# Two-layer hybrid decoder step: all heads two per bisection round, top-k rounds inside the projection, bias table flipped by DMA

## What is computed

```python
def mixer_ab(hn, attend, conv_buf, h0, w_in, w_out, conv_w, conv_b, wa, ba, wx, bx, lam):
    q, k, v, qi, ki, wi, g, xr = split_cols(hn @ w_in, AB_SPLITS)
    ...
    attn = attend(q, k, v, qi, ki, wi)
    rg, new_buf, h_last = rglru_branch(g, xr, conv_buf, h0, conv_w, conv_b, wa, ba, wx, bx, lam)
    return jnp.concatenate([attn, rg], axis=-1) @ w_out, k, v, ki, h_last, new_buf

def select_topk(scores, q_pos, k_pos, topk):
    admissible = k_pos[None, None, :] <= q_pos[None, :, None]
    _, idx = lax.top_k(jnp.where(admissible, scores, -jnp.inf), topk)
    ...

def gathered_attention(q, k_sel, v_sel, sel_pos, valid, q_pos, rel_bias):
    ...
    bias = rel_bias[t5_bucket(q_pos[None, :, None] - sel_pos)].astype(jnp.float32)
    logits = jnp.where(valid[:, :, None, None, :], logits + bias, -jnp.inf)
    p = jax.nn.softmax(logits, axis=-1).astype(v_sel.dtype)
    out = jnp.einsum('bqkgj,bqjkd->bqkgd', p, v_sel)

def rglru_branch(g, xr, buf, h0, conv_w, conv_b, wa, ba, wx, bx, lam):
    xc, new_buf = causal_dwconv(xr, buf, conv_w, conv_b)
    r = sigmoid(xb @ wa + ba); i = sigmoid(xb @ wx + bx)
    log_a = -RG_C * r * jax.nn.softplus(-lam.astype(jnp.float32))
    u = jnp.sqrt(-jnp.expm1(2.0 * log_a)) * (i * xc.astype(jnp.float32))
    hs, h_last = linear_recurrence(jnp.exp(log_a), u, h0.astype(jnp.float32))
    return jax.nn.gelu(g) * hs.astype(g.dtype), new_buf, h_last.astype(h0.dtype)
```

## Time and profile before

| | us |
|---|---|
| three executions | 1347.97, 1351.44, 1353.28; median 1351.44 |
| the profiled execution | 1351.15, its span 1349.4 |
| TensorE busy | 1256.8 (93%) |
| VectorE busy | 702.3 (52%) |
| ScalarE busy | 470.2 (35%) |
| GpSimd busy | 193.0 (14%) |

### The profile page before, as it was taken

The page is one execution under the profiler, slowest core; times in us unless marked ns, Lnnn a source line. Parts: engine busy times, 40 slices in busy tenths (PEclk is TensorE's granted clock), DMA queues, the critical chain, the costliest instruction groups (busy, mean ns, idle before and its releaser), DMA issues.

```text
span 1349.4 us, 24444 instructions
## 1 busy us (share of the span) xinstructions
PE 1256.8 (93%) x9991; PEld 1213.2 (90%) x9993; DVE 702.3 (52%) x1279; ACT 470.2 (35%) x548; POOL 193.0 (14%) x285
## 2 busy tenths in 40 slices
PE   5998994795999999999999999999999999999995
PEld 5878993563899999999999999999899999999994
DVE  5267786767347555555522244644755555552323
ACT  5243235451224434343322234332543343432110
POOL 0111001106303111111100010030411111110000
PEclk9999997696799999999999999999999999999998
DMA  7143301002222222222222332112122222222211
GB/s 271 64 149 123 132 33 46 1 2 65 68 93 70 89 91 93 93 93 93 87 89 109 102 125 94 64 64 93 63 94 93 93 93 93 93 86 87 86 60 63
DMA packets 25992, 118.17 MB, mean 88 GB/s; under 512 B 7720, under 2 KB 9192, under 8 KB 13904
## 3 DMA queue, kind: packets, MB, share of 16 engines
q1 hardware_dynamic: 21184, 105.50, 22.4%
q0 software_dynamic: 2048, 10.54, 2.3%
q10 hardware_dynamic: 2704, 1.35, 0.4%
HBM read 113.91 MB, written 3.46 MB: 87 GB/s over the span
## 4 chain that ended last, share of the span: by engine, by line
PE 70%; DVE 2%; POOL 1%; ACT 1%; issue 0%; DVEq 0%
PE ps L814 22%; PE ps L815 22%; PE ps L817 22%; POOL xl L1802 1%; PE ps L831 1%; PE ps L950 1%; PE ps L947 1%; PE ps L948 1%; PE ps L1209 0%; DVE acc L1240 0%; DVE vtc L1765 0%; DVE yt L1794 0%; PE ps L1121 0%; DVE rstd L1244 0%; DVE xn L1244 0%
## 5 line engine op out<-in xcount | busy, mean ns | idle before, releaser
L814 PE MATMUL ps<-xh,w_h 128*128 128x260 f32 x1792 | 471.4, 284 | 7.9 <-POOL xl L1802 7.8
L815 PE MATMUL ps<-xl,w_h 128*128 128x260 f32 x1792 | 469.6, 283 | 0.0
L817 PE MATMUL ps<-xh,w_l 128*128 128x260 f32 x1792 | 361.0, 283 | 0.0
L814 PEld LDWEIGHTS ps<-xh,w_h 128*128 128x128 f32 x1792 | 339.4, 189 | 9.1 <-issue 7.6
L815 PEld LDWEIGHTS ps<-xl,w_h 128*128 128x128 f32 x1792 | 338.8, 189 | 0.1
L1233 DVE TENSOR_TENSOR w_l<-w_raw,w_h 128x2048 fp32r<-128x2048 f32 (+1 forms) x94 | 211.6, 2251 | 166.4 <-ACT w_h L503 166.2
L817 PEld LDWEIGHTS ps<-xh,w_l 128*128 128x128 f32 x1792 | 277.1, 189 | 0.0
L815 PE MATMUL ps<-hl,w_h 128*128 128x260 f32 x704 | 183.9, 282 | 0.0
L503 ACT ACTIVATE w_h<-w_raw 128x2048 fp32r<-128x2048 f32 (+1 forms) x50 | 92.3, 1846 | 262.2 <-PE ps L817 242.4
L814 PE MATMUL ps<-hh,w_h 128*128 128x260 f32 x704 | 183.4, 282 | 0.0
L947 PE MATMUL ps<-xh,w_h 128*128 128x260 f32 x448 | 128.9, 309 | 14.1 <-DVE xl L1253 12.5
(11 more groups left out here) (298 smaller groups left out, 1406.3 us busy)
## 6 DMA issues: line engine op xcount, KB each, us to landing
w_raw<-in_wstream SPq DMA_DIRECT2D x86, 1024.0 KB, 4.8
w_raw<-in_wstream SPq DMA_DIRECT2D x8, 768.0 KB, 4.2
res<-in_x_t SPq DMA_DIRECT2D x4, 520.0 KB, 8.3
out_y<-yt SPq DMA_DIRECT2D x8, 260.0 KB, 2.2
tabf<-bias_by_distance SPq DMA_DIRECT2D x1, 2048.0 KB
wm<-in_sgu_w ACTq DMA_DIRECT2D x1, 512.0 KB, 3.6
sb_b<-in_sgu_b ACTq DMA_DIRECT2D x1, 512.0 KB, 4.2
out_f<-ost SPq DMA_DIRECT2D x2, 198.0 KB, 4.6
```

Of the source, the lines that this page charges most:

```text
L814: pe.matmul(out[h], wh, hi[h], start=(first and k == 0), stop=False)
L815: pe.matmul(out[h], wh, lo[h], start=False, stop=False)
L817: ins = pe.matmul(out[h], wl, hi[h], start=False, stop=(last and k == nk - 1))
```

## The change

- `ROUND`: rounds 9 to 24 have two heads each, 25 to 31 none. The wait for the logits of head 31 after the bisection goes.
- `p_work` on TensorE makes the next pair's logits first, then the turns and values.
- Rounds 0 to 7 get three matmuls on unused data behind the count (`warm`), into a PSUM bank that nobody reads.
- The shares of the recurrence move from rounds 2 to 5 to rounds 9 to 12, with ScalarE's rates; its root moves to round 17.
- All 48 top-k rounds lie inside groups 4 to 9. The page columns are split: their first half is made in group 6. The values are turned in group 9, step 12, and copied ahead of that group's last evacuation.
- The decay constants move from group 5 to group 1.
- The bias table is flipped by DMA: `fneg` is written to DRAM eight times per head, and sixteen reads fetch eight rows each, so the eight products, their copies, `flip` and `tabf` go. GpSimd no longer waits for the table at its start, nor for the gates ahead of its mask copies.

```diff
-        for rnd in range(17, 33):
-            ROUND[rnd] = (rnd - 1,)
+        for rnd in range(17, 25):
+            ROUND[rnd] = (2 * rnd - 18, 2 * rnd - 17)
...
-            sp.wait_ge(f_ev, 2)
-            sp.dma_start(scratch.ap(), fneg[:]).then_inc(d_scr, 16)
...
-                if s == 2:
-                    sp.wait_ge(d_scr, 16)
-                    sp.dma_start(tabf[:], bass.AP(scratch.ap().tensor, 0, [[1, P], [640, 8], [1, SEQ]])).then_inc(d_scr, 16)
+                if s == 3:
+                    sp.wait_ge(f_ev, 2)
+                    for h in range(2):
+                        sp.dma_start(bass.AP(scratch.ap().tensor, h * 8 * 640, [[2 * 8 * 640, 4], [640, 8], [1, 640]]),
+                                     fneg[4 * h:4 * h + 4, :].rearrange("p (a c) -> p a c", a=1).broadcast_to((4, 8, 640)))\
+                            .then_inc(d_scr, 16)
+                if s == 5:
+                    sp.wait_ge(d_scr, 32)
+                    for r in range(0, P, 8):
+                        sp.dma_start(tab[r:r + 8], bass.AP(scratch.ap().tensor, P - 1 - r,
+                                                           [[639, 8], [8 * 640, 8], [1, SEQ]])).then_inc(d_tabs, 16)
...
+                if g == 1:
                     act.wait_ge(sp_z, 1)
                     act.activation(lamt[:, 1, :], lamt[:, 0, :], ACT.Exp, scale=-1.0).then_inc(sp_e, 1)
...
-                    if g in (1, 2) and step % 4 == 3:
-                        table(4 * (g - 1) + step // 4)
...
+                if 9 <= rnd < 13:
+                    rates(rnd - 9)
+                if rnd == 17:
+                    roots()
...
+                if g == 9 and step == 12:
+                    turn_values()
...
             def p_work(rnd):
 
+                for i in heads(rnd + 1):
+                    if i % 2 == 0:
+                        p_pair(i // 2)
                 for i in heads(rnd - 1):
                     p_turn(i)
                 for i in heads(rnd - 2):
...
-                for i in heads(rnd + 1):
-                    if i % 2 == 0:
-                        p_pair(i // 2)
+            def warm():
+
+                for n in range(3):
+                    pe.matmul(ps[:, 3, :], sameb[:], pickb[NCH - 1][:], start=True, stop=True)
+
+            pe.wait_ge(topk_done, 3)
             for rnd in range(32):
                 count(rnd)
+                if rnd < 8:
+                    warm()
                 p_work(rnd)
...
-            rounds = {4: (0, 0, 3), 5: (4, 4, 2), 6: (4, 4, 2), 7: (4, 4, 2), 8: (0, 0, 0), 9: (4, 5, 0)}
+            rounds = {4: (0, 0, 3), 5: (4, 6, 2), 6: (4, 5, 2), 7: (4, 6, 3), 8: (0, 0, 2), 9: (4, 3, 0)}
...
-                if g == 5:
+                if g == 1:
                     decay_constants()
...
+                if g == 9:
+                    dve.wait_ge(vn_tr, 1)
+                    dve.wait_ge(d_kvi, 48)
+                    dve.tensor_copy(vn[:].rearrange("p n c -> p (n c)"), ps[:, 4, :]).then_inc(vn_ev, 1)
                 evac_b(g)
+                if g == 6:
+                    page_columns()
...
-            dve.wait_ge(vn_tr, 1)
-            dve.wait_ge(d_kvi, 48)
-            dve.tensor_copy(vn[:].rearrange("p n c -> p (n c)"), ps[:, 2, :]).then_inc(vn_ev, 1)
-            page_columns()
-            topk_rounds(q, 3 * ROUNDS - q)
+            page_terms_out()
...
-                if 2 <= rnd < 6:
-                    rg_share(rnd - 2)
+                if 9 <= rnd < 13:
+                    rg_share(rnd - 9)
...
-            p_logits(31)
```

More of the change, by code:

```diff
@@ L930, in beside, with turn_values @@
                         score_unit(u - 1)
+                if g == 9 and step == 12:
+                    turn_values()
+            def turn_values():
+                pe.wait_ge(ev_a, NUNITS_I - 1)
+                for n in range(NCH):
+                    ins = pe.transpose(ps[:, 4, n * P:(n + 1) * P], vt[:, n * P:(n + 1) * P], ident[:])
+                ins.then_inc(vn_tr, 1)
             def by_tiles(s, a_ready, b_ready, beside, g, x_wait=None):
@@ L974, in _ @@
                 ins.then_inc(gate_mm, 1)
-            for n in range(NCH):
-                ins = pe.transpose(ps[:, 2, n * P:(n + 1) * P], vt[:, n * P:(n + 1) * P], ident[:])
-            ins.then_inc(vn_tr, 1)
             pe.wait_ge(sig_done, 8)
@@ L1988 @@
     cols = lambda t: t.reshape(-1, P).T
-    ident, flip, dist, blocks, picks, slots, columns = shape_constants()
+    ident, dist, blocks, picks, slots, columns = shape_constants()
     rel4 = np.zeros((P, P), np.float32)
@@ L2014 @@
         "sgu_b0": np.repeat(a["sgu_b"][0, :, 0][None], P, axis=0),
-        "c_ident": ident, "c_flip": flip, "c_dist": dist, "c_blocks": blocks, "c_pick": picks, "c_slots": slots,
+        "c_ident": ident, "c_dist": dist, "c_blocks": blocks, "c_pick": picks, "c_slots": slots,
     }
```

39 lines of the change are left out of this document (14 added, 25 removed).

## The result

The changed kernel takes 1343.79 us (median of 7 runs, 1341.7 to 1344.35) beside 1351.04 us of the kernel before on the same chip; the ratio is 0.9945, 95% interval [0.9931, 0.9959]. That is 7.3 us less, where 24.1 were forecast and 1327.0 us given. The direction is right; the size is not, and the time lies outside the stated range (1320 to 1338).

A forecast was written before the change was run, and what follows sets the result against it. TensorE paces the input groups and the heads, VectorE and ScalarE the stretch from 209 to 238 us. The terms bring count 31 from 299.05 to 274.9, 24.1 us less than 1351.15: 1327.0 us, range 1320 to 1338.

The forecast's parts named there:

- The bias table: Groups 1 and 2: eight flip products leave TensorE, which never waits there, gaining 6.8 us.
- The decay constants: Group 5: with the constants in group 1, TensorE's wait and the low clock after it go, gaining 5.5 us.
- The top-k rounds: All 48 inside groups 4 to 9: group 8's first tile evacuated too late for TensorE by 1.1 us, between 0 and 2.5.
- the values: Their four transposes, now in group 9, put another 0.5 us on TensorE.
- Count 0: Start of the bisection: first count on TensorE at 208.3 us, behind the gates, with the samples' keys landing in time.
- Bare rounds: Nine rounds without heads at 0.96 us each, plus 0.9 (0 to 5) for GpSimd's products; count 9 at 217.8.
- Rounds 9 to 12: Two heads of block 0 and a recurrence share per round: 2.0 us a round, count 12 at 223.8.
- The heads: From count 12 TensorE is the bound: 45.0 us of products plus 2.3 for the root, ending at 271.1.
- The root: ScalarE's root with table loads in round 17 adds 2.3 us to the heads, between 0 and 4.5.
- The clock at 1.00 throughout: Granted clock of TensorE at the full level from count 0 near 208 until about 270.
- The rival of the first half: Clock falls in the bisection's first half: 1331 us if at round 9, 1338 if from round 0, 1333 taken; chance 0.20.
- The bare rounds behind: Rounds 27 to 31 come without heads after the heads end: 3.8 us that singles would have hidden, count 31 at 274.9.

The follow-up runs named there:

- e6: The change with the next pair's logits issued last again, behind turns, values and outputs of a round: 1332.4 us, ratio 0.9874 to the kernel before.
- e1: The change plus 20 filler products on TensorE in rounds 8 to 15: 1334.7 us, ratio 0.9880 to the kernel before.
- e14: The change with pairs issued last and with the filler products of e1: 1329.6 us, ratio 0.9861 to the kernel before.
- e9: e6 with the recurrence shares in rounds 4 to 7 and rates and root ahead of the heads: 1327.7 us, ratio 0.9829 to the kernel before.
- e2: The change with the shares back in rounds 2 to 5 and rates and root ahead of all heads: 1339.7 us, ratio 0.9922 to the kernel before.
- e10: e9 with one head per round in rounds 17 to 32: 1323.4 us, ratio 0.9797 to the kernel before.
- e13: The change with only a pair's first head issued ahead of the turns, the second behind the outputs: 1367.6 us, ratio 1.0134 to the kernel before.
- e3: The change with one head per round in rounds 17 to 32 (blocks 2 and 3): 1331.0 us, ratio 0.9853 to the kernel before.
- e5: The change without the warm products in rounds 0 to 7: 1342.7 us, ratio 0.9943 to the kernel before.
- e15: The change with the wait for the second head's bank put ahead of both heads' products: 1341.1 us, ratio 0.9930 to the kernel before.
- e4: The change's input groups and bisection start, with the whole bisection as in the kernel before: 1324.9 us, ratio 0.9802 to the kernel before.

## Why the prediction was wrong, step by step

1. **The bias table** (6.8): right, 6.8. The steps of groups 1 and 2 take 0.72 us throughout. SyncE's sixteen reads held TensorE nowhere.
2. **The decay constants** (5.5): right, 5.7. The index-key product of group 5 starts without a wait, at 1.00.
3. **The top-k rounds** (+1.1) and the values (+0.5): the late evacuation came, at 1.28 us of idleness (row at 176.81). That TensorE would then run at the half clock from 178 to 185 was not foreseen. It cost 3.1 us: at the start of group 9 TensorE was 12.5 us ahead of the kernel before (176.81 against 189.31), at the second tile of it only 9.4 (191.37 against 200.72). The last evacuation ended at 199.85 instead of 198.7. That it is no more than 1.1 us late is luck: TensorE was 1.5 us ahead already at the start of group 1 (30.74 against 32.19), which no term of the prediction holds, and the last evacuation followed the last product 0.6 us sooner. In e6, where the clock held and the lead at group 1 was 0.2 us, it ended at 198.04: the terms themselves were right within 0.7.
4. **Count 0** at 208.3: 209.43, all of it from step 3. The keys' reload behaved as said.
5. **Bare rounds** (0.96 each, +0.9): 0.97, 1.10, three of 1.24, then 0.96. The threshold update of one element took 0.73 us beside GpSimd's product, 0.15 without it (timeline of VectorE after):

```profile
211.35 0.73 DVE L1508 SCALAR_TENSOR_TENSOR sm<-sm 128x1 f32<-128x1 f32 x1
...
217.96 0.15 DVE L1508 SCALAR_TENSOR_TENSOR sm<-sm 128x1 f32<-128x1 f32 x1
```

GpSimd in the same time:

```profile
209.53 5.01 POOL L1871 TENSOR_TENSOR ii<-ii,xc 128x520 f32<-128x520 f32 x4 [9.30 <-ACT ii L593]
```

Three rounds lose 0.28 each and one 0.14, 1.0 us in all. The page "SBUF — State Buffer" of the Trainium skill (Practical consequences) names this contention; this trace agrees, and it is far from the upper bound of 5. Sticking out of the warm products: nothing.
6. **Rounds 9 to 12** (2.0 each): 1.70, 1.71, 3.17. Count 12 at 225.65 instead of 223.8, of which 1.1 are step 4's. The third round is the first at the half clock.
7. **The heads** (47.3 from count 12 to count 27): **61.1. This is the step that failed.** Three sizes in it were wrong.
 - "Issuing the logits of the next pair right behind the count, before the turns that wait for ScalarE, removes just these" 2.7 us of idle time. It closed a ring of waits instead, and cost 9 to 10 us (e6), of which about 2 remain where the clock is held up (e1 against e14). The step looked only at what the pair waits for and not at what is queued behind it: the turns, and through them ScalarE and VectorE.
 - The root, +2.3 between 0 and 4.5, cost 6.6 in its stretch (e6 against e9): TensorE was idle for 3.25 us and then worked 7 us at the half clock. With the pair first it cost 3.7 (the change against e2).
 - The clock at 1.00 throughout. It was down for 24 us and, behind the root, for some 3 more. The rival of the first half had this case, with 3.7 us if it fell at round 9; it fell at 222.6 in round 11. The 3.7 were too small: fillers alone gave 8.0 us back in rounds 9 to 16 (e1). The rule quoted there from the Trainium skill's page "TensorE: Matmul & The Clock Gate" (Part 4), that transposes do not count as busy in the same way, fits a clock that stays down at 22.60 of 23 us; but e6, with the same transposes in another order, rose at 228.7, so the rule alone does not explain it.
 With order and root undone, e9 needs 46.2 us from count 12 to count 27, 7 of them at the half clock, against 45.0 in the prediction for the products alone: that term was sound.
8. **The bare rounds behind** (3.8): 3.86. That pairing costs them without a return was said, and e10 measured 4.3.

The 15.7 us by which count 31 came late are then 1.1 of step 4, 0.7 in rounds 0 to 11 and 13.8 of step 7. What in the pair's order kept the clock down stays open.

## What to carry to other kernels

Before an instruction that waits is moved forward in an in-order queue, list what stands behind it and who waits for that, round the other engines, until the chain ends or closes; a closed chain can set the pace of the rounds, whatever the busy shares say. A cost that was counted at the full clock has to be counted a second time at the half one, and waits that are short at the one may close a ring at the other. Changes that come together are best priced against a version with each undone: here the four edits of the bisection, none of which helped, hid 19 of 26 us that the rest had gained.

## What the runs showed of the hardware

**A high busy share did not raise the clock.** TensorE in e13 was busy for 72.00 of 72 us and at 0.50 in all of them; the change was busy for 22.60 of 23 us at 0.50; e6, with the same products in another order, fell at 218.5 and rose at 228.7. All kernels with the pair first and no fillers rose for the heads only between 243 and 248 us (the change, e2, e3, e5, e15; e13 at 295), all with the pair last while block 1 was under way (e6 at 228.7, e9 and e10 at 233 and 235, e4 at 236). What in the order does it stays open: neither the parted products nor the idle time alone, since e13 had no idle time and e15 no parted products, and both stayed down.

**The same wait can cost nothing or 3 us.** Up to 186 us the change, e2, e3, e5 and e6 hold the same instructions on TensorE and the same idle time before the first tile of group 9, 1.27 or 1.28 us. The clock then stood at the lower level for about 7 us in the change (0.57 over 178 to 186), for 3 to 4 in e2, e3 and e5, and not at all in e6 (rows above), whose records show 68 products in those 8 us where the change's show 43. By the start of the second tile of group 9 that is 3.1 us between the change and e6; the 1.8 us at count 9 are what is left of it, since e6 had lost 1.3 us in its first group. So in a pair of single profiles a difference of 2 us ahead of count 9 tells nothing of the edits.

**Products of 64 rows go in pairs.** Two heads on different halves of the rows take 1.65 us together and 1.65 each when parted (384 columns, half clock), and 0.92 together (e9 in block 2) and 0.91 for the first alone (the row at 252.69 above) at the full one.
